# A two-block transformer kernel in float32: the weight sums of the second block's gate pairs made by accumulating transfers in place of GpSimd additions

## The reference, cut to what matters

```python
h = rmsnorm_2(x, pre_norm_g[l])
proj = h @ w_in[l]                    # u, v, z_a, c_q, ..., z_c, g_a, g_b, g_c
y_a = gmlp_spatial(...) * silu(z_a)
y_b = mla_attention(...) * silu(z_b)
y_c = rg_lru(...) * silu(z_c)
merged = (sigmoid(g_a) * (y_a @ w_proj_a[l])
          + sigmoid(g_b) * (y_b @ w_proj_b[l])
          + sigmoid(g_c) * (y_c @ w_proj_c[l]))
x = x + rmsnorm_2(merged @ w_out[l], post_norm_g[l])
```

## Time and profile before

| | us |
|---|---|
| median of three runs | 3142.2 (3142.07 to 3142.66) |
| the profiled execution, its own time | 3142.73 |
| its span | 3141.4 |

### The profile page before, as it was taken

One profiled execution on the slowest core, in us unless ns is written; L12 is line 12 of the kernel. 1 busy time (PEld: TensorE's weight loads), 2 busy tenths in 40 slices (PEclk: granted clock), 3 DMA queues, 4 the chain that ended last, 5 costly groups with the idle time before them and its releaser, 6 DMA issues.

```text
span 3141.4 us, 38508 instructions
## 1 busy us (share of the span) xinstructions
PE 3129.8 (100%) x15416; PEld 2644.8 (84%) x15416; DVE 1953.5 (62%) x2640; ACT 1316.9 (42%) x2059; POOL 546.5 (17%) x395
## 2 busy tenths in 40 slices
PE   9999999999999999999999999999999999999999
PEld 8888888888888888888887888888888788888887
DVE  6876456565687655665558744457756764455774
ACT  4333334344433334343445532236745543233762
POOL 1201212110020111111013210130221321131031
PEclk9999999999999999999999999999999999999999
DMA  4322323235443233222652233223442222223423
GB/s 169 117 99 96 98 97 107 95 115 199 149 121 99 90 101 114 94 94 96 206 171 83 79 97 102 86 98 112 127 168 97 82 97 95 94 88 101 137 96 136
DMA packets 105906, 353.71 MB, mean 113 GB/s; under 512 B 13888, under 2 KB 14144, under 8 KB 104448
## 3 DMA queue, kind: packets, MB, share of 16 engines
q1 hardware_dynamic: 101856, 328.47, 32.0%
q0 software_dynamic: 3728, 22.25, 1.9%
q10 hardware_dynamic: 144, 0.52, 0.1%
HBM read 328.64 MB, written 6.29 MB: 107 GB/s over the span
## 4 chain that ended last, share of the span: by engine, by line
PE 95%; DVE 3%; ACT 1%; DMA 0%; SPq 0%; issue 0%; POOL 0%; POOLq 0%
PE ps L632 94%; DVE r L1750 1%; DVE wl L1740 1%; PE ps L723 1%; PE ps L1014 0%; DVE f L1755 0%; SPq L2666 0%; DVE f L1818 0%; DMA X<-x_in 0%; DMA f<-f 0%; DVE f L2053 0%; DVE r L2232 0%; ACT wh L1147 0%; ACT f L1560 0%; DVE sm L2258 0%; PE ps L676 0%
## 5 line engine op out<-in xcount | busy, mean ns | idle before, releaser
L632 PE MATMUL ps<-h,wh 128*128 128x512 f32 (+1 forms) x5696 | 1609.5, 368 | 0.7
L632 PEld LDWEIGHTS ps<-h,wh 128*128 128x128 f32 x5696 | 1029.8, 188 | 182.8 <-issue 3.4
L632 PE MATMUL ps<-h,wl 128*128 128x512 f32 (+1 forms) x2848 | 1046.1, 367 | 0.0
L1740 DVE TENSOR_TENSOR wl<-raw,wh 128x1024 fp32r<-128x1024 f32 (+2 forms) x551 | 681.9, 1248 | 265.3 <-ACT wh L1147 264.7
L1147 ACT CAST wh<-raw 128x1024 fp32r<-128x1024 f32 (+3 forms) x564 | 557.7, 1004 | 441.0 <-PE ps L632 436.7
L632 PEld LDWEIGHTS ps<-h,wl 128*128 128x128 f32 x2848 | 534.6, 188 | 88.6
L632 PE MATMUL ps<-r,wh 128*128 128x512 f32 x1536 | 474.8, 390 | 3.0 <-DVE f L2276 2.0
L632 PEld LDWEIGHTS ps<-r,wh 128*128 128x128 f32 x1536 | 284.6, 188 | 62.4 <-issue 2.9
L1244 ACT CAST r<-f 128x512 fp32r<-128x512 f32 x194 | 119.4, 622 | 511.5 <-DVE f L2151 149.0
L632 PE MATMUL ps<-r,wl 128*128 128x512 f32 x792 | 304.3, 389 | 0.0
L632 PE MATMUL ps<-wh,r 128*128 128x512 f32 x960 | 302.5, 390 | 0.2
(11 more groups left out here) (193 smaller groups left out, 2846.5 us busy)
## 6 DMA issues: line engine op xcount, KB each, us to landing
raw<-wst SPq DMA_DIRECT2D x544, 512.0 KB, 3.3
raw<-wst SPq DMA_DIRECT2D x48, 320.0 KB, 2.9
r<-r SPq DMA_DIRECT2D x64, 128.0 KB, 2.3
f<-gains POOLq DMA_DIRECT2D x6, 1024.0 KB, 5.2
raw<-wst SPq DMA_DIRECT2D x20, 256.0 KB, 2.9
f<-f SPq DMA_DIRECT2D x72, 64.0 KB, 2.0
f<-tab POOLq DMA_DIRECT2D x16, 256.0 KB, 5.0
kept_x<-X POOLq DMA_DIRECT2D x2, 2048.0 KB, 9.2
```

Of the source, the lines that this page charges most:

```text
L632: return e.matmul(o, a, b, start=start, stop=stop, skip_group_check=True)
L1740: e.tensor_tensor(l[:, 0:WIDTH[c]], sources(c)[0], h[:, 0:WIDTH[c]].bitcast(F32), ALU.subtract).then_inc(*lo_cut.up(("lo", c)))
```

## The change

The sums are no longer made on GpSimd. The weights of a pair are read a second time from `wst`, by DMA issued on GpSimd's queue: a plain transfer writes W into the sum's tile, and a transfer with `accum_op=ALU.add` adds the next W to it. S0, S1 and S3 are now one tile in succession (`sum_at(name, 0)`), S2 is another (`sum_at(name, 2)`). A pair has six transfers of 128x512, in three steps:

- `sums_begin`: a plain transfer into each of the two tiles;
- `sums`: waits for each of these to land, and adds: now S0 and S2 are there;
- `sums_more`: waits until VectorE has cut S0 (`*0`, second half), adds for S1 in the same tile; waits until VectorE has cut S1, adds for S3.

ScalarE's and VectorE's waits name the same events as before, which are now signalled by the landing of these transfers. A pair's first two steps stand in GpSimd's program ahead of the last step of the pair before. A `raw` buffer is released as soon as its last half is cut (`released`). For b, `sums_more` of b5 stands behind the first of four `layer_norm` steps.

```diff
@@ released
-    return ("sums", CHUNKS[c][0][:-2], 3), ("lo", c + 2)
+    return (("lo", c + 2 if r not in RAW_OF else c + 1, 0),)
@@ sum_at, sums_free
+def sum_at(name, q):
+    n = PAIR_J[name[6]].index(int(name[8])) % 2
+    return SUMS_AT[name[6]][n + 2 if q == 2 else n]
-def sums_free(name, q):
+def sums_free(name, third):
     L, nm, j = int(name[0]), name[6], int(name[8])
-    if j != PAIR_J[nm][0]:
-        return ("lo", NAME[f"{name[:8]}{j - 2}*{q}"])
-    c = ("done", ("ri", L, 9)) if q else ("done", ("pr", L, "a", 7))
+    n = PAIR_J[nm].index(j)
+    if n > 1:
+        return ("lo", NAME[f"{name[:8]}{PAIR_J[nm][n - 2]}*{2 if third else 3}"])
+    c = ("done", ("ri", L, 9)) if third or n else ("done", ("pr", L, "a", 7))
@@ gpsimd
+            def sums_begin(name):
+                r, n = RAW_OF[NAME[f"{name}*0"]], PAIR_J[name[6]].index(int(name[8])) % 2
+                w.wait_ge(*at(*sums_free(name, False)))
+                e.dma_start(F(sum_at(name, 0)), wst[r, :, 0:S]).then_inc(*sum_done[n].up(("sum_begun", name)))
+                w.wait_ge(*at(*sums_free(name, True)))
+                e.dma_start(F(sum_at(name, 2)), wst[r + 1, :, 0:S]).then_inc(*third_done[n].up(("third_begun", name)))
             def sums(name):
-                r, t = RAW_OF[NAME[f"{name}*0"]], [F(i) for i in SUMS_AT[name[6]]]
-                one, two = raw[:, r % NRAW, :], raw[:, (r + 1) % NRAW, :]
-                w.wait_ge(s_raw[r % NRAW], 16 * (r // NRAW + 1))
-                w.wait_ge(s_raw[(r + 1) % NRAW], 16 * ((r + 1) // NRAW + 1))
-                for q, (a, b) in enumerate(((one[:, 0:S], two[:, 0:S]), (t[0], two[:, S:2 * S]), (two[:, 0:S], two[:, S:2 * S]),
-                                            (t[1], one[:, S:2 * S]))):
-                    w.wait_ge(*at(*sums_free(name, q)))
-                    if q in (1, 3):
-                        w.wait_ge(*at("sums", name, q // 2))
-                    e.tensor_tensor(t[q], a, b, ALU.add).then_inc(*pool_tile.up(("sums", name, q)))
+                c, n = NAME[f"{name}*0"], PAIR_J[name[6]].index(int(name[8])) % 2
+                r, t = RAW_OF[c], F(sum_at(name, 0))
+                w.wait_ge(*at("sum_begun", name))
+                e.dma_start(t, wst[r + 1, :, 0:S], accum_op=ALU.add).then_inc(*sum_done[n].up(("sums", name, 0)))
+                w.wait_ge(*at("third_begun", name))
+                e.dma_start(F(sum_at(name, 2)), wst[r + 1, :, S:2 * S], accum_op=ALU.add).then_inc(
+                    *third_done[n].up(("sums", name, 2)))
+            def sums_more(name):
+                c, n = NAME[f"{name}*0"], PAIR_J[name[6]].index(int(name[8])) % 2
+                r, t = RAW_OF[c], F(sum_at(name, 0))
+                w.wait_ge(*at("lo", c, 1))
+                e.dma_start(t, wst[r + 1, :, S:2 * S], accum_op=ALU.add).then_inc(*sum_done[n].up(("sums", name, 1)))
+                w.wait_ge(*at("lo", c + 1, 1))
+                e.dma_start(t, wst[r, :, S:2 * S], accum_op=ALU.add).then_inc(*sum_done[n].up(("sums", name, 3)))
...
+                for j in PAIR_J["b"]:
+                    sums_begin(f"{L}/gateb_{j}")
                 sums(f"{L}/gateb_3")
                 sums(f"{L}/gateb_5")
-                for i in range(4):
+                sums_more(f"{L}/gateb_3")
+                small_step("layer_norm", L, 0)
+                sums_more(f"{L}/gateb_5")
+                for i in range(1, 4):
                     small_step("layer_norm", L, i)
...
                 for b in "ac":
-                    for j in PAIR_J[b]:
+                    for j in (2, 4):
+                        sums_begin(f"{L}/gate{b}_{j}")
+                    for j in (2, 4):
                         sums(f"{L}/gate{b}_{j}")
-                        if j > 2:
-                            add_gated(L, b, (j - 4, j - 3))
+                    sums_more(f"{L}/gate{b}_2")
+                    sums_begin(f"{L}/gate{b}_6")
+                    sums(f"{L}/gate{b}_6")
+                    for j in (4, 6):
+                        sums_more(f"{L}/gate{b}_{j}")
+                        add_gated(L, b, (j - 4, j - 3))
                     add_gated(L, b, (4, 5, 6, 7))
```

More of the change, by code:

```diff
@@ L546, in sources @@
                 return [raw[:, r % NRAW, 0:WIDTH[c]]]
-            t = F(SUMS_AT[CHUNKS[c][0][6]][q])
+            t = F(sum_at(CHUNKS[c][0][:-2], q))
             return [raw[:, (r + q // 2) % NRAW, (S if q else 0):(2 * S if q else S)], t] if q < 3 else [t]
@@ L594, in build @@
                    dve_col, pool_tile, pool_sum, pool_col]
+        sum_done, third_done = ([Signal(sem(f"s_{what}{i}"), 16) for i in range(2)] for what in ("sum", "third"))
         swap_done = [Signal(sem(f"s_swap{r}"), 16) for r in range(5)]
@@ L597, in build @@
         far_done = [Signal(sem(f"s_far{t}"), 16) for t in range(5)]
-        signals += swap_done + list(spread_done.values()) + far_done
+        signals += sum_done + third_done + swap_done + list(spread_done.values()) + far_done
         loads = {}
```

## The result

The changed kernel takes 3224.2 us (3221.9 to 3227.1), the kernel before 3142.3 in the same session: a ratio of 1.0261 [1.0248, 1.0273], 81.9 us slower. The forecast was 3186 with a range of 3160 to 3226: the direction and the mechanism hold, the size is 38 us short, and the time lies at the upper edge of the range. The forecast's own range (3167 to 3210) does not hold it.

A forecast was written before the change was run, and what follows sets the result against it. TensorE bounds the kernel, busy 3129.8 of 3141.4 us. Added stalls 25.4 + 14.0 + 1.0 + 3.4 = 43.8 us put the median of 3142.2 at 3186; range 3160 to 3226, own range 3167 to 3210.

The forecast's parts named there:

- a2, 4a - 4.1: Pair a2: four landings in a row delay n5 and u2, a stall of 12.7 us a layer, 25.4 in two.
- a: Time of one transfer from issue to landing, taken as 4.2 us for all steps; lower bound 3.2, above 5.1 or 7.
- c4 and c6, 2a - 4.9: Pairs c4 and c6: two landings behind VectorE's cuts delay u2 by 3.5 us each, 14.0 in two layers.
- c2: Pair c2: second plain transfer waits for the LRU's last gate product; 0.5 us a layer, 1.0 in all, between nothing and 3.
- b5, a4, a6: Later pairs begun early, two landings left: stall 2a - 8.5 at a6, the others within 0.4 us; none at 4.2.
- b3: Pair b3: far more room than the other later pairs, so no stall; a stall there would show the forecast wrong.
- clock: TensorE slow after idleness: 17 fewer matmuls, 1.7 us, behind a2's long stall in each layer; 3.4 us in all.
- slow accumulation: Rival, chance 0.2: a of 5.1 or more, every pair but b3 stalls; 3213 us at 5.1, 3275 at 7.
- What goes is worth nothing: GpSimd's 64 additions, 100.6 us busy, and earlier release of raw buffers save nothing, since nobody on the path waits.
- Quick transfers: Rival, chance 0.13: a of 3.2 or below, no c2 or clock term; 3166 us, or 3156 at 2.6.
- Not slower: Rival, chance 0.07: freed VectorE gains 0.26 us at a2 in two layers, transfers hidden; 3142 us, needs a at most 1.0.
- Doesn't do what it says: Rival, chance 0.02: GpSimd issues a2's first transfers early, or p1's copy isn't held; 2a - 4.1 a layer, about 3166 us.

The follow-up runs named there:

- the filled waits: Changed kernel with matmuls that nothing reads in TensorE's waits: at a2 alone 3222.7 us; at a2, c2, c4 and c6 3214.4 us.

## Why the prediction was right in kind and short in size

The terms, as forecast and as the profile after has them, in two layers:

| term | forecast | measured | short by |
|---|---|---|---|
| a2, 4a - 4.1 | 25.4 | 16.6 + 15.2 = 31.8 | 6.4 |
| c4 and c6, 2a - 4.9 | 14.0 | 4.78 + 3.79 + 4.48 + 4.02 = 17.1 | 3.1 |
| c2 | 1.0 | 9.0 | 8.0 |
| b5, a4, a6 | 0 | 2.05 + 0.69 + 0.78 = 3.5 | 3.5 |
| b3 | 0 | 0 | 0 |
| clock | 3.4 | 20.2 | 16.8 |
| sum | 43.8 | 81.6 | 37.8 |

The stated range holds the time by 1.8 us, and the same program measured again, at 3227.6, lies outside it. Its upper end was drawn for slow accumulation, while the two largest shortfalls are c2 and the clock; that it held is in part luck.

**What goes is worth nothing.** Right: with the additions back the time is that of before within 3.3 us, and VectorE's subtractions at a2, 0.69 us now, stand beside no gain.

**The chain at a2, and its form.** Right. The three signs that it named are there: 4.9 us ahead of n5 for VectorE's subtraction, a longer wait ahead of u2 for ScalarE's copy, and casts of sums that wait for DMA. By hand from the product's end at 2027.55: the four steps of 21.1 us and the fixed 4.4 give 2053.0, and u2 starts at 2054.2. One hand-over is long enough for the rest: VectorE is done with S0 at 2037.33, and GpSimd issues S1 at 2039.01. Its last issue for a4 had ended at 2037.09; what held it then no row names. At the other three a2 in the two profiles of this kernel the hand-over takes 0.54 to 0.75 us.

**The size of a.** Wrong by 1.1 us a step at the first a2, where 4.2 was taken and 5.3 measured (21.1 / 4), and by 0.8 at the second (20.0 / 4). The choice weighed two rows of plain transfers. It left out that an accumulating one occupies GpSimd for 0.87 us instead of 0.54, and that accumulation costs time where a transfer goes alone on its queue too: S1 and S3 land after 4.9 and 4.2 us by median, and after 3.3 and 3.2 without it. With plain transfers, for which the rows stood, a is 3.5 and the formulas fit within 1 us.

**The later pairs.** c4 and c6 are as forecast with a of 4.8 (5.37 and 4.24 at c4, from the issues at 2295.43 and 2302.64 to the casts at 2300.80 and 2306.88). b5, a4 and a6, whose stall was to begin at 4.25, stay between 0 and 2.05. b3 has none, as said.

**c2** is the step that failed in kind: 4.8 and 4.2 us where 0.5 was taken and 3 was the bound. The working stopped at the first accumulation. S1's transfer, behind VectorE's cut of S0, lands at 2271.50 after 4.98 us, and ScalarE comes to the copy of p1 only at 2274.60, so u2 starts 2.15 us late. The copies stand ahead of S3 here, which saves u2 from that one landing only, and S3's cast then holds the product's chunk behind it. ScalarE at c2, the cast of S3 and that of the product's chunk:

```profile
2278.25 0.62 ACT L1160 CAST wh<-f 128x512 fp32r<-128x512 f32 x1 [3.00 <-DMA f<-wst]
2278.78 0.72 ACT L1155 CAST wh<-raw 128x640 fp32r<-128x640 f32 x1
```

The product tile at 2280.45 waits for it, 2.33 us. The experiment with the copies moved ahead made this pattern at every pair.

**The clock** is the term that was most mis-sized. It was priced from the opening of the kernel, once per a2, at 1.7 us. There the granted clock reads 1.00 while the matmuls go at half pace, so this row alone could not say that the clock is what falls. That 1.00 was misread: the trace before has its first record of the clock at 6.6 us, and a stretch without a record is printed as 1.00. After the change the first record stands at 4.1 us, and the matmuls quicken there:

```profile
2.00:4.00 2.00, 2.00 (x11) 2.00 (x10) 0.00 (x0) 0.47 (x1) 0.00 (x0) 1.00 0.87 221
4.00:6.00 2.00, 2.00 (x19) 2.00 (x19) 0.00 (x0) 0.00 (x0) 0.00 (x0) 1.00 0.85 266
```

The profile after does say it: 0.50 to 0.51 behind the stalls. It falls at both parts of a2, at c4, c6 and once in c2, ten times in two layers, which makes 2 us each. By the rule from the Trainium skill (TensorE: Matmul & The Clock Gate, Part 1) that the prediction weighed, the throttled state is the default and activity releases it; by that rule, the trace after agrees, with 0.213 in place of 0.118 us per matmul. That the slow matmuls come from idleness is shown by the filled waits: clock 1.00 across a2, and 13 us back in branches a and c together.

**The rivals.** Slow accumulation (3213 at a = 5.1) is nearest in time, and at a2 it is the case that came: a was 5.3. But its further stalls at b5, a4 and a6 mostly failed to come (3.5 us, not 10.2), and of the 38 us that are missing, c2 makes a fifth and the clock more than two fifths, and neither comes from its formulas. Quick transfers (3.2 or below) fall: no accumulating one landed before 3.7 us, and only some plain ones by 3.2. "Not slower" decided from a = 1.0 on, and no transfer came near that. "Doesn't do what it says" falls: GpSimd issues a2's first transfer at 2027.49, behind the last product, and p1's copy stands behind the cast at 2053.28. The Trainium skill's fit for a transfer (DMA: Bandwidth & Descriptors, "Anatomy of one DMA — SWDGE (gpsimd) path"), 2.6 us, is below the plain transfers here too, 3.3 to 3.6 us by median, and well below the accumulating ones, 4.2 to 5.8.

## What to carry to other kernels

Work taken off an engine that nobody waits for is worth nothing, and its replacement must be priced by latency: a chain of landings, each behind another engine's cut, costs a step apiece on the first consumer that comes soon. Add to each stall of TensorE of a few us the half pace behind it, here a quarter of the whole loss; and follow a waiting cast to everything queued behind it, not only to the first instruction that is known to need it.

## What the runs showed of the hardware

- An accumulating transfer of 256 KB occupies GpSimd 0.87 to 0.93 us at its issue, a plain one 0.54 to 0.56, and lands after 4.2 to 5.8 us by median against 3.3 to 3.6. Without accumulation the same 96 transfers land after 3.5 by median and the kernel is 35 us faster.
- Landings scatter: the first accumulations lie between 4.0 and 10.9 us, and one program's time varies by 6 us within a session where the kernel before stays within 2.
- Behind each of the eight stalls of 3.8 to 11.7 us TensorE was granted 0.50 of its clock for some us, and so behind two at c2 of 2.33 and 2.37, but not behind the one of 2.15 there. With plain transfers it fell behind a wait of 1.90 us (at 2318.15) and not behind one of 1.96 (at 2292.40). The length of the stall alone does not say it.
- GpSimd stood idle ahead of some issues with no releaser named, 2.13 us at 2036.22. The cause is open; it was not tried.
